# HGRN products of a head in eight small heaps behind half chunks instead of four behind whole chunks

## The chip, the cores and the metric

The kernel runs on one core of one Trainium2 chip. The metric is the device time of one execution in microseconds (us), median over runs; lower is better. TensorE (PE in the rows) does the matmuls, VectorE (DVE), ScalarE (ACT) and GpSimd (POOL) the elementwise work, and SyncE (SP) issues the large transfers.

## The reference, cut to what matters

The reference is one step of a two-layer decoder trunk over 512 prompt tokens and 8 sample tokens (520 columns, two halves of 260). The change touches one of its blocks, the HGRN2 mixer of the second layer: a projection to q, f, i and g, a gated linear recurrence with a 128x128 state for each of 8 heads, a norm and an output projection.

```python
def hgrn2_mixer(x, s0, lb, w_in, norm_g, w_out):
    proj = (x @ w_in).astype(f32)
    q, fz, i_in, g = jnp.split(proj, [HG_WIDTH, 2 * HG_WIDTH, 2 * HG_WIDTH + HG_HEADS * HG_DV], axis=-1)
    q = jax.nn.silu(q)
    logf = jnp.logaddexp(jnp.log(lbf), jnp.log1p(-lbf) + jax.nn.log_sigmoid(fz))
    k = -jnp.expm1(logf)
    o, s_fin = hgrn2_chunked(heads(q, HG_DK), heads(k, HG_DK), heads(i_in, HG_DV), heads(logf, HG_DK), s0)
    o = rmsnorm(o, norm_g).reshape(bsz, t, HG_HEADS * HG_DV) * jax.nn.silu(g)
    return o.astype(x.dtype) @ w_out, s_fin.astype(s0.dtype)
...
def step(s, inp):
    bcum = jnp.cumsum(gc, axis=1)
    o_inter = jnp.einsum('bthk,bhkv->bthv', qc * jnp.exp(bcum), s)
    att = jnp.einsum('bthk,bshk,btshk->bhts', qc, kc, decay)
    o_intra = jnp.einsum('bhts,bshv->bthv', att, vc)
    k_dec = kc * jnp.exp(btot[:, None] - bcum)
    s_new = jnp.exp(btot)[..., None] * s + jnp.einsum('bshk,bshv->bhkv', k_dec, vc)
```

`step` is the body of `hgrn2_chunked`, run over 8 chunks of 64 tokens with the state carried from one to the next.

## The kernel before

All activations lie feature by token. A projection is done in **chunks** of 128 output features; `chunk` (L2490 and on) does the two token halves of a chunk, 8 k-tiles with 3 matmuls of 260 columns each (high times high, low times high, high times low part), so 24 matmuls per half and 48 per chunk, into one of two pairs of PSUM banks (`lin`, j = 0 or 1). Before a chunk starts, its weights must be loaded (SP), copied to `w_hi` (ACT, `split`) and subtracted to `w_lo` (DVE, `split`, counted in `lo_ready`), and the last result in its banks must be taken out (`used[j]`).

In the HGRN block the engines each run a loop `hg_in` over h, written by hand as one straight program. Step h projects head h in four chunks, which give f, q, i and g in that order (DVE takes them out at L1896 to `t`, L1929 to `hgQ`, L1963 to `hgV` and L1998 to `hgG`). Beside this it does the products of head g = h-1 and the last ones of head e = h-2. These products are plain fp32 matmuls in **groups**, each filling one PSUM bank of `mis`:

- V, K: transposes of i and of the decayed k, copied out by ACT (L1487).
- S: the sample tokens' outputs, 8 matmuls with one column each.
- A0 to A3: q times k inside blocks of 32, 16 and 8 tokens and on the diagonal (L2378 three times, L2384), put under a mask into `attn` by DVE (L1918).
- D0, D1: k times v for 8 blocks of 64 tokens, from which DVE forms the running state `hS` in a chain of 8 steps (L1969, L1973).
- B0, B1: v of the sample tokens, spread, which DVE adds to the states `sS` (L1986).
- O: the output (L2393, L2399), copied out by ACT (L1530).
- N: sums of squares for the norm, one column each. R, r: the root spread over partitions, multiplied in by DVE (L1889).

**The order of groups** is the list `made` for `HG`, and PE must fill them in this order. There are four banks, used in turn: `Groups.reuse` makes PE wait before group q until group q-4 has been taken out by its owner (`void_dve` or `void_act`). PE's program puts the groups behind whole chunks: S and A0 to A3 behind the first, V, K, N behind the second, D and B behind the third, O, R, r behind the fourth. A run of groups between projection matmuls is called a **heap** here. DVE and ACT take the groups out at fixed places of their own straight programs. For h = 8 and 9 there is no projection left and the groups follow each other directly; the output projection (`hg_out`) comes after.

Of the kernel before, what the change touches and what calls it, by code (L numbers as in the profile page):

```python
# [12 lines left out]
P = 128  # L13
# [114 lines left out]
def trunk_kernel(nc, i_, o_):  # L128
# [408 lines left out]
    for h in range(HH + 2):  # L537
        g, e = h - 1, h - 2
        if 0 <= e < HH:
            made += [("S", e, "dve")]  # L540
        if 0 <= g < HH:
            made += [("A", (g, u), "dve") for u in range(len(LEVELS) + 1)] + [("V", g, "act"), ("K", g, "act")]
        if 0 <= e < HH:
            made += [("N", e, "act")]
        if 0 <= g < HH:
            made += [("D", (g, 0), "dve"), ("D", (g, 1), "dve"), ("B", (g, 0), "dve"), ("B", (g, 1), "dve")]
            made += [("O", g, "act")]
        if 0 <= e < HH:
            made += [("R", e, "dve"), ("r", e, "dve")]
    HG = Groups(made, hg["fill"], {"dve": hg["void_dve"], "act": hg["void_act"]}, banks=4)  # L550

# [85 lines left out]
    with block:  # L637
# [565 lines left out]
        def _(act):  # L1203
# [246 lines left out]
            def hg_in():  # L1450
# [3 lines left out]
                for h in range(HH + 3):  # L1454
                    g, e, d, p, b = h - 1, h - 2, h - 3, p0 + 2 * h, h % 2
                    if h < HH:
                        split(p, 1, KD)
                        if h == 0:
                            root(norm_of["hg_in", 1])
                            act.wait_ge(hg["lb"], 1)  # L1460
                        act.wait_ge(used[0], p + 1)
                        wait(act, gated, 2 * h)
                        if h >= 2:
                            act.wait_ge(hg["s_state"], 2 * (h - 1))
                            act.wait_ge(hg["scaled_pool"], POOLS * (h - 1))
                            act.wait_ge(hg["scaled_dve"], h - 1)
                        act.activation(hgF[:], t3[:], ACT.Sigmoid)
                        act.activation(hgK[b][:], t3[:], ACT.Sigmoid, scale=-1.0).then_inc(f_out, 1)
# [9 lines left out]
                    if h < HH:  # L1478
# [3 lines left out]
                        split(p + 1, 1, KD)  # L1482
                    if 0 <= g < HH:
                        for what, dst in (("V", vTok), ("K", kTok)):
                            q = G.at(what, g)
                            act.wait_ge(hg["fill"], q + 1)
                            act.activation(dst[:].rearrange("p a b -> p (a b)"), hg_bank(q), ACT.Copy)\  # L1487
                                .then_inc(hg["void_act"], 1)
                    if 0 <= e < HH:
# [85 lines left out]
        def _(dve):  # L1575
# [298 lines left out]
            def hg_in():  # L1874
# [3 lines left out]
                def halves(t, level):  # L1878
                    return t.rearrange("p q (b a t) -> p q b a t", a=2, t=level)[:, :, :, 1, :]

                for h in range(HH + 3):
                    g, e, d, p, b = h - 1, h - 2, h - 3, p0 + 2 * h, h % 2
# [18 lines left out]
                    if 0 <= g < HH:  # L1901
                        if g:
                            dve.wait_ge(hg["fill"], G.at("O", g - 1) + 1)
                        else:
                            dve.wait_ge(hg["consts"], 1)
                        for u, level in enumerate(LEVELS + (None,)):
                            q = G.at("A", (g, u))
                            dve.wait_ge(hg["fill"], q + 1)
                            if u:
                                dve.wait_ge(hg["void_dve"], G.before(q, "dve"))  # L1910
                            m = pair_mask[:, u:u + 1, :].bitcast(I32)
                            if level is None:
                                dst, src, m = attn[:], hg_bank(q).rearrange("p (q t) -> p q t", q=4), m.to_broadcast([P, 4, P])
                            else:
                                dst, m = halves(attn[:], level), halves(m, level)
                                m = m.to_broadcast([P, 4, P // (2 * level), level])
                                src = hg_bank(q)[:, 0:SEQ // 2].rearrange("p (q b t) -> p q b t", q=4, t=level)
                            dve.copy_predicated(dst, m, src).then_inc(hg["void_dve"], 1)  # L1918
                    if 0 <= e < HH:
# [3 lines left out]
                    if h < HH:  # L1923
# [9 lines left out]
                        dve.wait_ge(gate_out, g0 + 2 * h + 1)  # L1933
                        dve.tensor_tensor(hgQ[b][:], hgQ[b][:], t2[:], ALU.mult).then_inc(gated, 1)
                    if 0 <= e < HH:
                        G.emptied_of(dve, "N", e)
# [6 lines left out]
                    if h < HH:  # L1943
                        split(p + 1, 1, KD)
                        dve.wait_ge(hg["log"], h + 1)
                        if h:
# [133 lines left out]
        def _(pe):  # L2080
# [362 lines left out]
            def hg_in(chunk):  # L2443

                p0 = first_pair["hg_in", 1]
                for h in range(HH + 2):
                    g, e, p = h - 1, h - 2, p0 + 2 * h
                    if h < HH:
                        chunk(p, 0, h == 0)
                    if h == 0:  # L2450
                        pe.wait_ge(kv_ev2, KV * DEPTH)
                    if 0 <= e < HH:
                        hg_group("S", e)
                    if 0 <= g < HH:
                        for u in range(len(LEVELS) + 1):
                            hg_group("A", (g, u))
                    if h < HH:
                        chunk(p, 1, False)
                    if 0 <= g < HH:
                        hg_group("V", g)  # L2460
                        hg_group("K", g)
                    if 0 <= e < HH:
                        hg_group("N", e)
                    if h < HH:
                        chunk(p + 1, 0, False)
                    if 0 <= g < HH:
                        for what in ("D", "B"):
                            for f in range(2):
                                hg_group(what, (g, f))
                    if h < HH:  # L2470
                        chunk(p + 1, 1, False)
                    if 0 <= g < HH:
                        hg_group("O", g)
                    if 0 <= e < HH:
                        hg_group("R", e)
                        hg_group("r", e)
                HG.all_emptied(pe, len(HG.groups))

            def stream(n):
# [9 lines left out]

                def chunk(p, j, first):  # L2490
                    pe.wait_ge(lo_ready, 2 * p + j + 1)
                    wait(pe, used[j], p)
                    for half in range(2):
                        cols = slice(half * HT, (half + 1) * HT)
                        for k in range(kt):
                            if first and half == 0:
                                pe.wait_ge(x_done, x0 + k + 1)
                            for u, (w, x) in enumerate(((w_hi, x_hi), (w_hi, x_lo), (w_lo, x_hi))):
                                ins = pe.matmul(lin[:, j, half, 0:HT], w[:, j, k, :], x[:, k, cols],  # L2499
                                                start=k == 0 and u == 0, stop=k == kt - 1 and u == 2)  # L2500
                    ins.then_inc(chunk_done, 1)
                    if first and r == 0:
# [57 lines left out]
```

## Time and profile before

| | us |
|---|---|
| median of 3 runs | 2648.4 |
| lowest, highest run | 2644.25, 2656.82 |
| the profiled execution | 2662.53 |
| its span in the trace | 2660.8 |
| TensorE busy | 2537.1 |
| VectorE busy | 1267.4 |
| ScalarE busy | 829.8 |
| GpSimd busy | 610.9 |
| mean granted TensorE clock | 0.968 |

The profiled execution is one execution; its trace covers its span, which is 1.7 us shorter than its own time. The HGRN block's projections start at 1708.92 us of the span, and `hg_out` starts at 2042.84. The granted clock is the share of full TensorE speed that the chip grants: 1.00 is 2.4 GHz, 0.50 is 1.2 GHz.

### The profile page before, as it was taken

What the parts mean: (1) busy time and instruction counts of PE and PEld (TensorE: products, weight loads), DVE (VectorE), ACT (ScalarE), POOL (GpSimd) and SP (SyncE); (2) the same over time, 40 slices, a digit from 0 to 9 for tenths busy, and PEclk for the clock granted to TensorE, in tenths of its full rate; (3) what the DMA queues carried; (4) which work ended last, traced back from release to release, by engine and by line L of the source; (5) the groups of instructions that cost most, each with busy time, mean ns of one, the idle gap of its engine ahead of it and who ended that gap; (6) DMA issues with size and microseconds to landing.
All of it is one profiled execution on the core that took longest, in us unless ns stands there. A gap on an engine that the chain in (4) does not pass through costs nothing.

```text
span 2660.8 us, 48881 instructions
## 1 busy us (share of the span) xinstructions
PE 2537.1 (95%) x20589; PEld 2447.2 (92%) x20589; DVE 1267.4 (48%) x1783; ACT 829.8 (31%) x1196; POOL 610.9 (23%) x604
## 2 busy tenths in 40 slices
PE   6999999888989999999999999999999999999998
PEld 6999998777976999999999999999999968999997
DVE  4553543924445543344443344556655564442444
ACT  3322231433222322222332233355544232221221
POOL 5588747230201100002111011222211203000002
PEclk8999999899989999999999999998988999999998
DMA  7245444452364233233443333232231543332331
GB/s 156 80 158 127 121 120 130 133 169 76 92 216 126 85 90 103 81 97 114 125 120 104 97 95 111 82 89 82 66 89 50 163 169 97 91 101 84 88 101 65
DMA packets 479667, 289.10 MB, mean 109 GB/s; under 512 B 22352, under 2 KB 467024, under 8 KB 478480
## 3 DMA queue, kind: packets, MB, share of 16 engines
q1 hardware_dynamic: 473760, 280.66, 35.9%
q0 software_dynamic: 848, 1.89, 0.7%
q10 hardware_dynamic: 4896, 4.20, 0.5%
q8 instruction: 124, 2.03, 0.3%
q14 instruction: 39, 0.32, 0.0%
HBM read 258.86 MB, written 27.85 MB: 108 GB/s over the span
## 4 chain that ended last, share of the span: by engine, by line
PE 86%; DVE 7%; ACT 3%; DMA 2%; issue 2%; POOL 0%; SPq 0%; ACTq 0%; POOLq 0%; DVEq 0%
PE lin L2499 70%; PE mis L2124 3%; DVE w_lo L1583 1%; PE mis L2378 1%; ACT w_hi L1212 1%; DMA raw<-in_s_w_glu_dram 1%; DVE rstd L1596 1%; PE mis L2243 1%; PE mis L2228 1%; DVE a_lo L1589 1%; PE mis L2421 1%; DMA raw<-in_xattn_w_q_dram 1%; PE mis L2178 1%; PE lin L2243 1%; PE mis L2384 1%
## 5 line engine op out<-in xcount | busy, mean ns | idle before, releaser
L2499 PE MATMUL lin<-a_hi,w_hi 128*128 128x260 f32 x3584 | 1029.0, 287 | 39.1 <-DVE w_lo L1583 34.7
L2499 PE MATMUL lin<-a_lo,w_hi 128*128 128x260 f32 x3584 | 1019.5, 284 | 0.0
L2499 PE MATMUL lin<-a_hi,w_lo 128*128 128x260 f32 x3584 | 1018.8, 284 | 0.0
L2499 PEld LDWEIGHTS lin<-a_hi,w_hi 128*128 128x128 f32 x3584 | 682.8, 191 | 46.8 <-DVE w_lo L1583 31.9
L1583 DVE TENSOR_TENSOR w_lo<-raw,w_hi 128x1024 fp32r<-128x1024 f32 (+1 forms) x328 | 496.3, 1513 | 436.8 <-ACT w_hi L1212 434.7
L2499 PEld LDWEIGHTS lin<-a_lo,w_hi 128*128 128x128 f32 x3584 | 683.1, 191 | 0.2
L2499 PEld LDWEIGHTS lin<-a_hi,w_lo 128*128 128x128 f32 x3584 | 683.0, 191 | 0.0
L2499 PE MATMUL lin<-h_hi,w_hi 128*128 128x260 f32 x2048 | 580.8, 284 | 8.2 <-DVE h_lo L1805 3.3
L2499 PE MATMUL lin<-h_hi,w_lo 128*128 128x260 f32 x2048 | 580.1, 283 | 0.0
L2499 PE MATMUL lin<-h_lo,w_hi 128*128 128x260 f32 x2048 | 579.4, 283 | 0.0
L1212 ACT ACTIVATE w_hi<-raw 128x1024 fp32r<-128x1024 f32 (+1 forms) x328 | 364.3, 1111 | 343.5 <-PE lin L2499 304.9
L2499 PEld LDWEIGHTS lin<-h_hi,w_hi 128*128 128x128 f32 x2048 | 387.8, 189 | 10.8 <-issue 6.0
L2499 PEld LDWEIGHTS lin<-h_hi,w_lo 128*128 128x128 f32 x2048 | 387.7, 189 | 0.0
L2499 PEld LDWEIGHTS lin<-h_lo,w_hi 128*128 128x128 f32 x2048 | 387.4, 189 | 0.0
L968 POOL TENSOR_TENSOR acc<-xT 128x520 f32<-128x520 f32 x8 | 9.8, 1224 | 966.2 <-DVE xT L2047 923.3
L2047 DVE SCALAR_TENSOR_TENSOR xT<-lin,xT 128x520 f32<-128x520 f32 (+1 forms) x88 | 61.5, 699 | 302.2 <-PE lin L2499 302.2
L1547 ACT ACTIVATE h_hi<-t 128x520 fp32r<-128x520 f32 (+1 forms) x88 | 56.2, 639 | 433.5 <-DVE t L2031 433.5
L1544 ACT ACTIVATE t<-t 128x520 f32<-128x520 f32 x88 | 56.5, 642 | 308.0 <-DVE t L2025 308.0
L2029 DVE TENSOR_TENSOR t<-lin,rstd 128x520 f32<-128x520 f32 x88 | 61.5, 699 | 177.2 <-PE lin L2499 177.2
L970 POOL TENSOR_TENSOR sqt<-xT 128x520 f32 (+1 forms) x56 | 74.5, 1330 | 254.5 <-DVE xT L2047 186.2
L2025 DVE TENSOR_TENSOR t<-lin,rstd 128x520 f32<-128x520 f32 x88 | 61.5, 699 | 108.4 <-PE lin L2499 108.2
L1221 ACT ACTIVATE a_hi<-xT,vec 128x520 fp32r<-128x520 f32 (+1 forms) x56 | 40.2, 729 | 230.4 <-DVE xT L2047 198.7
(429 smaller groups left out, 2670.8 us busy)
## 6 DMA issues: line engine op xcount, KB each, us to landing
raw<-in_ffn_w_in_dram SPq DMA_DIRECT2D x176, 512.0 KB, 3.8
raw<-in_ffn_w_out_dram SPq DMA_DIRECT2D x64, 704.0 KB, 4.6
kc<-in_cache_mem_k_dram SPq DMA_DIRECT2D x32, 512.0 KB, 4.9
vc<-in_cache_mem_v_dram SPq DMA_DIRECT2D x16, 1024.0 KB, 7.3
raw<-in_hg_w_in_dram SPq DMA_DIRECT2D x32, 512.0 KB, 4.0
raw<-in_xattn_w_kv_dram SPq DMA_DIRECT2D x16, 512.0 KB, 4.1
raw<-in_s_w_glu_dram SPq DMA_DIRECT2D x16, 512.0 KB, 4.2
raw<-in_xattn_w_q_dram SPq DMA_DIRECT2D x16, 512.0 KB, 4.7
```

Source lines behind the costliest of these rows:

```text
L970: step.link(pool.tensor_tensor(sqt[:], tile(xT, m), tile(xT, m), ALU.mult))
L1212: act.activation(w_hi[:, j, 0:kt, :], raw[:, j, 0:kt, :], ACT.Copy).then_inc(hi_ready, 1)
L1221: act.activation(tile(a_hi, m), tile(xT, m), ACT.Copy, scale=vec[:, bass.ds(row + m, 1)]).then_inc(a_hi_done, 1)
L1544: act.activation(t2[:], t1[:], ACT.Silu).then_inc(gate_out, 1)
L1547: act.activation(tile(h_hi, i), t3[:], ACT.Copy).then_inc(h_hi_done, 1)
L1583: dve.tensor_tensor(w_lo[:, j, 0:kt, :], raw[:, j, 0:kt, :], w_hi[:, j, 0:kt, :].bitcast(F32), ALU.subtract).then_inc(lo_ready, 1)
L2025: dve.tensor_tensor(two(t1[:]), lslot(0), two(rstd[:]), ALU.mult).then_inc(used[0], 1)
L2029: step.link(dve.tensor_tensor(two(t4[:]), lslot(1), two(rstd[:]), ALU.mult))
L2047: dve.scalar_tensor_tensor(out=twotile(xT, m), in0=lslot(j), scalar=scale, in1=twotile(xT, m), op0=ALU.mult, op1=ALU.add)\
L2124: ins = pe.matmul(kv_bank(c)[:, 0:NM], w[:, e, k, :], x[:, k, :], start=k == 0 and u == 0, stop=k == KD - 1 and u == 2)
L2243: ins = pe.matmul(bank, vM[layer][:, m, (2 * h + e) * P:(2 * h + e + 1) * P], pT[:, h % 2, m, :], start=m == 0, stop=m == 1)
L2499: ins = pe.matmul(lin[:, j, half, 0:HT], w[:, j, k, :], x[:, k, cols], start=k == 0 and u == 0, stop=k == kt - 1 and u == 2)
```

## The change

PE's loop now places groups behind half chunks. `chunk` takes the halves to do, waits for weights and banks only with the first, and counts the chunk as done only with the second. The order of groups becomes V, K | S | A0, A1 | A2, N | A3, D0, D1 | B0, B1 | R, r | O, in eight heaps behind the eight halves of a step. Along with it ACT copies V and K out at the start of its step, ahead of the sigmoids of f, and DVE does the mask copies of A0 and A1 where all four stood, that of A2 after q is gated and that of A3 ahead of the clamp of log f. The number of matmuls, copies, banks and transfers is the same.

```diff
@@ made, the order of groups
     for h in range(HH + 2):
         g, e = h - 1, h - 2
+        if 0 <= g < HH:
+            made += [("V", g, "act"), ("K", g, "act")]
         if 0 <= e < HH:
             made += [("S", e, "dve")]
         if 0 <= g < HH:
-            made += [("A", (g, u), "dve") for u in range(len(LEVELS) + 1)] + [("V", g, "act"), ("K", g, "act")]
+            made += [("A", (g, u), "dve") for u in range(len(LEVELS))]
         if 0 <= e < HH:
             made += [("N", e, "act")]
         if 0 <= g < HH:
+            made += [("A", (g, len(LEVELS)), "dve")]
             made += [("D", (g, 0), "dve"), ("D", (g, 1), "dve"), ("B", (g, 0), "dve"), ("B", (g, 1), "dve")]
-            made += [("O", g, "act")]
         if 0 <= e < HH:
             made += [("R", e, "dve"), ("r", e, "dve")]
+        if 0 <= g < HH:
+            made += [("O", g, "act")]
...
@@ ACT, hg_in
                     if h < HH:
                         split(p, 1, KD)
+                    if 0 <= g < HH:
+                        for what, dst in (("V", vTok), ("K", kTok)):
+                            q = G.at(what, g)
+                            act.wait_ge(hg["fill"], q + 1)
...
@@ DVE, hg_in (causal(g, u) is the old body of the loop over u)
-                        for u, level in enumerate(LEVELS + (None,)):
...
+                        for u in range(2):
+                            causal(g, u)
...
                         dve.tensor_tensor(hgQ[b][:], hgQ[b][:], t2[:], ALU.mult).then_inc(gated, 1)
+                    if 0 <= g < HH:
+                        causal(g, 2)
...
                     if h < HH:
                         split(p + 1, 1, KD)
+                    if 0 <= g < HH:
+                        causal(g, 3)
+                    if h < HH:
                         dve.wait_ge(hg["log"], h + 1)
...
@@ PE, hg_in (mine: 0 <= g < HH, older: 0 <= e < HH)
+                    def projected(i, half):
+                        if h < HH:
+                            chunk(p + i // 2, i % 2, h == 0 and i == 0, (half,))
...
+                    projected(0, 0)
+                    if mine:
+                        hg_group("V", g)
+                        hg_group("K", g)
+                    projected(0, 1)
+                    if older:
+                        hg_group("S", e)
+                    projected(1, 0)
+                    if mine:
+                        hg_group("A", (g, 0))
+                        hg_group("A", (g, 1))
+                    projected(1, 1)
+                    if mine:
+                        hg_group("A", (g, 2))
+                    if older:
                         hg_group("N", e)
+                    projected(2, 0)
+                    if mine:
+                        hg_group("A", (g, 3))
+                        hg_group("D", (g, 0))
+                        hg_group("D", (g, 1))
+                    projected(2, 1)
+                    if mine:
+                        hg_group("B", (g, 0))
+                        hg_group("B", (g, 1))
+                    projected(3, 0)
+                    if older:
                         hg_group("R", e)
                         hg_group("r", e)
+                    projected(3, 1)
+                    if mine:
+                        hg_group("O", g)
...
@@ chunk
+                def chunk(p, j, first, halves=(0, 1)):
+                    if 0 in halves:
+                        pe.wait_ge(lo_ready, 2 * p + j + 1)
+                        wait(pe, used[j], p)
+                    for half in halves:
...
+                    if 1 not in halves:
+                        return
                     ins.then_inc(chunk_done, 1)
```

Two places of the compiled order follow. On PE, in the step of a middle head, before the change the S group (matmuls on `hgQ` and `sS`) and all four A groups stand in one heap between projection matmuls on `a_hi`, `a_lo`:

```order
L2499 MATMUL lin<-a_hi,w_lo 128x260
L2426 MATMUL mis<-hgQ_140,sS_157 128x1 x8
L2378 MATMUL mis<-lvl_160 128x64 x4
L2378 MATMUL mis<-lvl_161 128x64 x4
L2378 MATMUL mis<-lvl_162 128x64 x4
L2384 MATMUL mis<-dgQ,dgK 128x128 x4
L2499 MATMUL lin<-a_hi,w_hi 128x260
```

With the change, in the same place, 24 projection matmuls (one half, left out as "...") lie between S, A0 with A1, and A2 with N:

```order
L2440 MATMUL mis<-hgQ_141,sS_158 128x1 x8
...
L2392 MATMUL mis<-lvl_160 128x64 x4
L2392 MATMUL mis<-lvl_161 128x64 x4
...
L2392 MATMUL mis<-lvl_162 128x64 x4
L2446 MATMUL mis<-ones,hgS 128x1 x4
L2446 MATMUL mis<-ones,hgS 8x1
...
L2398 MATMUL mis<-dgQ,dgK 128x128 x4
```

The heap of S and A0 to A3 has become four heaps with projection between them, the last of them shared with D0 and D1.

On ACT, before the change the copies of V and K (`vTok`, `kTok`) stand between the sigmoid of q with the split behind it and the root, scaling and logarithm that end in `bC`:

```order
L1481 ACTIVATE t_64<-hgQ_140 128x520
L1212 ACTIVATE w_hi<-raw 128x1024
L1487 ACTIVATE vTok<-mis 128x512
L1487 ACTIVATE kTok<-mis 128x512
L1494 ACT_TABLE_LOAD
L1494 ACTIVATE rT<-mis,eps 128x4
L1495 ACTIVATE rT<-mis,eps 8x1
L1499 ACTIVATE hgK_142<-hgK_142,lbv 128x520
L1501 ACT_TABLE_LOAD
L1501 ACTIVATE bC<-hgF,lbv 128x512
```

With the change they stand at the start of the step, behind the copy of the last head's output (`hO`) and the split for the second chunk:

```order
L1535 ACTIVATE hO<-mis 128x512
L1216 ACTIVATE w_hi<-raw 128x1024
L1466 ACTIVATE vTok<-mis 128x512
L1466 ACTIVATE kTok<-mis 128x512
L1478 ACTIVATE hgF<-t_65 128x520
L1479 ACTIVATE hgK_142<-t_65 128x520
```

The stretch from the sigmoid of q to `bC` has become shorter by two copies. The copy of `hO`, which waits for group O, still stands ahead of the split for the second chunk, while group O itself has moved to the end of PE's step.

## Rows read from the trace of the kernel before

**Rows 1.** The page: granted clock in tenths of full speed, 40 equal slices of the span.
```profile
PEclk8999999899989999999999999998988999999998
```

**Rows 2.** Busy by stretch (start:end length, busy, counts, PEclk, DMA): whole head steps.
```profile
1730.00:1765.00 35.00, 35.00 (x300) 34.74 (x299) 24.00 (x41) 22.80 (x38) 15.91 (x15) 1.00 0.28 79
1765.48:1806.55 41.07, 41.07 (x324) 40.62 (x324) 23.78 (x50) 21.46 (x36) 8.49 (x9) 0.92 0.28 79
...
1929.58:1970.57 40.99, 40.99 (x324) 40.55 (x323) 24.56 (x51) 21.90 (x37) 7.68 (x9) 0.92 0.29 80
```

**Rows 3.** The same view: stretches of low clock, first and last shown, six in all.
```profile
1774.00:1780.80 6.80, 6.80 (x34) 6.80 (x33) 2.68 (x5) 0.99 (x2) 0.00 (x0) 0.50 0.46 128
...
1978.90:1985.60 6.70, 6.70 (x33) 6.70 (x33) 2.20 (x5) 1.59 (x3) 0.00 (x0) 0.50 0.35 97
```

**Rows 4.** The same view: D, B; O, R, r; the steps without projections.
```profile
1834.50:1838.00 3.50, 3.50 (x34) 3.37 (x33) 3.14 (x7) 3.48 (x11) 0.00 (x0) 1.00 0.53 150
1843.80:1847.50 3.70, 3.70 (x34) 3.58 (x32) 3.15 (x10) 0.60 (x1) 3.70 (x3) 1.00 0.06 18
...
2007.00:2047.00 40.00, 36.50 (x226) 35.37 (x225) 20.88 (x52) 12.74 (x26) 4.82 (x4) 0.70 0.15 44
```

**Rows 5.** Chain that ended last (start, length, what), step of h = 1.
```profile
1737.95 2.62 PE mis L2378 x24
1740.58 0.95 PE mis L2384 x8
1741.52 5.73 PE lin L2499 x48
```

**Rows 6.** The same view, step of h = 3.
```profile
1812.55 1.68 PE mis L2426 x16
1814.22 4.45 PE mis L2378 x24
1818.68 1.81 PE mis L2384 x8
1820.49 6.39 PE lin L2499 x48
1826.88 0.87 PE mis L2408 x8
1827.75 0.91 PE mis L2432 x10
1828.66 5.92 PE lin L2499 x48
```

**Rows 7.** Instructions in order of time (start, length, engine, line), DVE, step of h = 4.
```profile
1867.91 0.70 DVE L1929 TENSOR_TENSOR hgQ<-lin,rstd 128x520 f32<-128x520 f32 x1 [3.71 <-PE lin L2499]
...
1875.67 0.43 DVE L1948 TENSOR_SCALAR bC<-bC 128x512 f32<-128x512 f32 x1 [0.79 <-ACT bC L1501]
...
1884.54 1.22 DVE L1583 TENSOR_TENSOR w_lo<-raw,w_hi 128x1024 fp32r<-128x1024 f32 x1 [0.24 <-DVE hS L1973]
```

**Rows 8.** The same view, ACT, from the same step.
```profile
1850.14 0.58 ACT L1530 ACTIVATE hO<-mis 128x512 f32<-128x512 f32 x1
1850.62 1.05 ACT L1212 ACTIVATE w_hi<-raw 128x1024 fp32r<-128x1024 f32 x1
...
1870.13 0.57 ACT L1487 ACTIVATE vTok<-mis 128x512 f32<-128x512 f32 x1
...
1871.21 1.28 ACT L1494 ACT_TABLE_LOAD   x1
```

**Rows 9.** The same view, PE: the first matmuls of a chunk behind a heap, full clock.
```profile
1741.28 0.37 PE L2499 MATMUL lin<-a_hi,w_hi 128*128 128x260 f32 x1
1741.48 0.28 PE L2499 MATMUL lin<-a_lo,w_hi 128*128 128x260 f32 x1
1741.60 0.28 PE L2499 MATMUL lin<-a_hi,w_lo 128*128 128x260 f32 x1
```

**Rows 10.** The same view, POOL, from the step of h = 4: outK scaled.
```profile
1886.31 1.26 POOL L1179 TENSOR_TENSOR outK<-outK,hgK 128x512 f32<-128x512 f32 x1
```

More of the change, by code:

```diff
@@ L1457, in hg_in @@
                         split(p, 1, KD)
+                    if 0 <= g < HH:
+                        for what, dst in (("V", vTok), ("K", kTok)):
+                            q = G.at(what, g)
+                            act.wait_ge(hg["fill"], q + 1)
+                            act.activation(dst[:].rearrange("p a b -> p (a b)"), hg_bank(q), ACT.Copy)\
+                                .then_inc(hg["void_act"], 1)
+                    if h < HH:
                         if h == 0:
@@ L1482, in hg_in @@
                         split(p + 1, 1, KD)
[L1483 to L1488, printed above, removed]
                     if 0 <= e < HH:
@@ L1879, in halves, with causal @@
                     return t.rearrange("p q (b a t) -> p q b a t", a=2, t=level)[:, :, :, 1, :]
+                def causal(g, u):
+                    q = G.at("A", (g, u))
+                    dve.wait_ge(hg["fill"], q + 1)
+                    if u:
+                        dve.wait_ge(hg["void_dve"], G.before(q, "dve"))
+                    m = pair_mask[:, u:u + 1, :].bitcast(I32)
+                    if u == len(LEVELS):
+                        dst, src, m = attn[:], hg_bank(q).rearrange("p (q t) -> p q t", q=4), m.to_broadcast([P, 4, P])
+                    else:
+                        level = LEVELS[u]
+                        dst, m = halves(attn[:], level), halves(m, level)
+                        m = m.to_broadcast([P, 4, P // (2 * level), level])
+                        src = hg_bank(q)[:, 0:SEQ // 2].rearrange("p (q b t) -> p q b t", q=4, t=level)
+                    dve.copy_predicated(dst, m, src).then_inc(hg["void_dve"], 1)
                 for h in range(HH + 3):
@@ L1905, in hg_in @@
                             dve.wait_ge(hg["consts"], 1)
-                        for u, level in enumerate(LEVELS + (None,)):
[L1907 to L1918, printed above, removed]
+                        for u in range(2):
+                            causal(g, u)
                     if 0 <= e < HH:
@@ L2447, in hg_in @@
                     g, e, p = h - 1, h - 2, p0 + 2 * h
[L2448 to L2458, printed above, removed]
@@ L2459, in hg_in @@
-                    if 0 <= g < HH:
+                    mine, older = 0 <= g < HH, 0 <= e < HH
+                    def projected(i, half):
+                        if h < HH:
+                            chunk(p + i // 2, i % 2, h == 0 and i == 0, (half,))
+                            if h == 0 and i == 0 and half == 1:
+                                pe.wait_ge(kv_ev2, KV * DEPTH)
+                    projected(0, 0)
+                    if mine:
                         hg_group("V", g)
                         hg_group("K", g)
-                    if 0 <= e < HH:
-                        hg_group("N", e)
@@ L2464, in hg_in @@
[L2464 to L2474, printed above, removed]
+                    projected(0, 1)
@@ L2488, in stream @@
                     x_done, x0 = a_lo_done, KD * split_norms.index(r_in)
[L2490 to L2493, printed above, removed]
+                def chunk(p, j, first, halves=(0, 1)):
[3 more added lines that the diff above has]
+                    for half in halves:
                         cols = slice(half * HT, (half + 1) * HT)
```

## The prediction

> **What bounds the kernel now.** I read the clock over the span first: it is below full speed in the slices of the HGRN block too, though these are full of work [rows 1]. Then the busy time by head step. The reader should see two things there. TensorE is busy for all of a step (41.07 of 41.07 us, 40.99 of 40.99), so no other engine holds it up; and its mean granted clock is 0.92, against 1.00 in the step of h = 1, which has no S heap yet [rows 2]. Cut finer, each step of h = 2 to 7 has one stretch of about 6.8 us at 0.50, that is at 1.2 GHz instead of 2.4, six in all, about 41 us apart [rows 3]. It begins inside the heap of S and A0 to A3. What TensorE did before it fell: 1.68 us of matmuls with one column each and then matmuls of 64 columns, behind a chunk at full clock [rows 6]. It fell behind no other heap of a step: D with B kept 1.00 for 3.5 us, O with R and r for 3.7 us [rows 4], and in the step of h = 1 A0 to A3 without S kept it too [rows 2]. So it takes thin and very thin products together to make it fall, and it is TensorE's own time, at a clock that it loses once a head, that bounds this block.
>
> The price of one fall is read by setting the same work at either clock side by side: the three levels of A 4.45 us against 2.62, the diagonal 1.81 against 0.95, the chunk behind it 6.39 against 5.73 [rows 5, 6]. That is 1.83 + 0.86 + 0.66 = 3.35 us. A step without it would be 41.0 - 3.3 = 37.7 us.
>
> **Part 1, the clock.** The change puts a half chunk, 2.9 us of dense matmuls (half of 5.8), between S (1.7 us) and A0 with A1 (two thirds of 2.62, 1.75 us), and again ahead of A2 with N (0.87 + 1.0 us). The thinnest heap is now S alone or N with A2, under 1.9 us, with dense work on both sides. V, K and N in one heap of 1.8 us, N's 0.91 us of single columns in it [rows 6], did not bring the clock down in these steps, and A without S, 2.62 + 0.95 us in the step of h = 1, did not either [rows 2, 5]. S alone is nearly twice N's length, and no row shows it alone between chunks; the nearest row is V, K, N, and I take no fall. Saved: six falls at 3.3 us, 19.8 us. The bounds are 0 (each head still falls once) and 19.8. The two steps without projections (h = 8, 9; mean clock 0.70 [rows 4]) keep their thin groups back to back, so their falls stay.
>
> The Trainium skill, "TensorE: Matmul & The Clock Gate", section "HAM oscillation — how this bites in real kernels", puts the fall of the clock down to idle gaps of TensorE. The trace differs: TensorE shows no idle time in steps whose clock falls [rows 2, 3]. By that rule alone nothing is there for the change to mend, and the first term would be 0; this is rival 2 below.
>
> **Part 2, more seams.** The first matmul of a chunk behind a heap takes 0.20 us to the next one's start, the second 0.12 [rows 9], so a seam costs 0.08 us, the way back into the heap I put at nothing or the same again. Four more seams in a step are 0.3 to 0.6 us; I take 0.4, and in the seven steps with heaps and chunks 2.8 us.
>
> **Part 3, a new wait for R.** With four banks R takes the bank of D0, which comes free only when DVE has finished the whole chain of `hS`. From the take-out of q to the clamp of log f are 7.76 us (1867.91 to 1875.67), from there to the end of the chain 8.87 (1884.54) [rows 7]. ACT's copies of V and K, 1.08 us (1870.13 to 1871.21), leave the first stretch [rows 8]; the mask copy of A3, 0.7 us, comes into DVE's part of it but fits in the 0.79 us for which DVE waited there [rows 7], and A3 itself is filled just in time: behind the second chunk come A2, N, half a chunk and A3 (0.9 + 1.0 + 3.0 + 0.9 = 5.8 us), while the logarithm comes 6.7 us behind q. So the bank is free 15.55 us after q, 15.75 after the second chunk's end (0.2 us from the end of a chunk to DVE's start). TensorE wants it after A2, N, half, A3 with D, half, B, half: 0.87 + 0.95 + 2.95 + 2.5 + 2.95 + 1.85 + 2.95 = 15.0, with seams 15.1. It waits 0.6 us. Bounds: 0, if 0.6 us of the chain goes; 1.5 if the split for g's weights and A3's copy come late.
>
> **Part 4, a new wait for K.** K takes the bank of R, which DVE empties behind the split for the second chunk, which needs ACT's `w_hi`, which stands behind ACT's copy of O. O now ends PE's step. From there: 0.25 us to ACT, the copy of O 0.5 and `w_hi` 1.0 (starts 1850.14, 1850.62, length 1.05 [rows 8]), the split 1.15, the product with R 0.7, together 3.65 to 3.7. PE has half a chunk and V, 2.95 + 0.45 = 3.4. It waits 0.3 us. Behind K in PE's queue stands the second half of the f chunk, so DVE's take-out of f and the sigmoids behind it move by the same 0.3 us. K's other input, outK scaled by POOL, came 19.7 us behind the take-out of q (1887.57 less 1867.91) [rows 7, 10]; K is now wanted 15.1 us (to R) + 1.3 + 2.95 + 2.4 + 2.95 + 0.45 = 25.2 us behind it, so 5 us of TensorE's own work hide that it is wanted earlier; with that cover gone each us would cost one per head.
>
> The two waits come from one loop, from the second chunk's end over `hS` to the next second chunk, so they are paid in each of the six steps: 0.9 x 6 = 5.4 us. Bounds 0 and 1.8 x 6 = 10.8.
>
> **Part 5, the rest.** DMAs are the same, SP's sample states wait for S, which now ends 0.9 us later in the step, with a step's time of cover. POOL's work is unchanged and waits for ACT only. The steps without projections hold the same chain V, K, A, D, B, O, then S, N, R in 35 us, in a new order; I put them at 0, with 2 us either way.
>
> **Sum for the profiled execution.** 2662.5 - 19.8 + 2.8 + 5.4 = 2650.9 us, a step of 37.7 + 0.4 + 0.9 = 39.0 us.
>
> **From there to a median.** The profiled execution is 14.1 us above the median and above all three runs, which themselves spread by 12.6 us. One fall is 3.3 us, so the spread is about four falls. One trace does not show how near to the edge they are; I read the spread as heads with and without a fall: the profiled execution had six of six, the median run fewer. Time that the timed runs lack for this reason cannot be saved again. If all 14.1 us are falls (4 of 6), the changed kernel's median is 2650.9; if none is, and it is what the profiling adds, it is 2636.8. The spread speaks for falls, and I take two thirds: 2650.9 - 4.9 = 2646.0. So the forecast is no difference that can be told, because what is saved in the falls is partly absent from the timed runs and partly paid back in seams and waits. A measurement of this kernel can tell about 0.5%, 13.2 us, from no change.
>
> **Rivals.**
> 1. The falls go and the waits do not come (the chain from q to `hS` 1 us shorter than I put it). A step is 38.1 us; 5.4 us less: 2640.6, and down to 2631.4 if the 14.1 us are profiling. For it: 0.6 and 0.3 us are small differences of sums of 15 and 4 us. Against: all their terms are rows.
> 2. **Slower:** the clock still falls once a head, at S or at one of the new seams, while seams and waits are paid. Its place is S with the half chunks around it; the price is the 2.8 + 5.4 = 8.2 us of parts 2 to 4, with nothing saved for it; against the profiled execution it decides once fewer than three of the six falls go (three are 9.9 us). Own time 2662.5 + 8.2 = 2670.7, median by the same two thirds 2665.8 at most, 2657 if the falls only stay as they are. For it: S's single columns last 1.7 us; also, the skill's page named above, section "A second HAM failure mode: psum-queue depth-cycling", says that waits between groups that cycle through PSUM banks make the clock go up and down, and the change adds two such waits. Against: V, K, N with single columns, and the trace's seams, without a fall [rows 4, 6]. I put it at 2664.
> 3. The falls go, and the loop of the two waits is 1.8 us a head, at the upper bound: 5.4 us more, 2651.4.
> 4. The saving is whole against the median, with waits as forecast: the profiled execution's 14.1 us are profiling, the timed runs had all their falls: 2637. For it: the clock stretches repeat so evenly. Against: three runs 12.6 us apart.
>
> That the change does not do what it says is excluded by the compiled order: S and the A groups are apart on TensorE.
>
> **How the numbers follow.** Forecast 0.42 (2640 to 2653), rival 1 0.13, rival 2 0.12, rival 3 0.11, rival 4 0.22. Faster by over 0.5% means under 2635.2: two fifths of rival 4, two fifths of rival 1 and 0.10 of the forecast, since the runs of before in the comparison may themselves lie high: together 0.24. Slower means over 2661.6, most of rival 2: 0.10. The rest, 0.66, is within 0.5%. The range runs from 2633, inside rivals 1 and 4, to 2659, the lower part of rival 2.
>
> **What the changed profile would show.** Right: no stretch at 0.50 between the start of the projections and the end of the seventh head's step, head steps of 38.5 to 39.5 us, TensorE idle ahead of R for about 0.6 us (released by DVE's `hS`) and ahead of K for 0.3 (by DVE's product with R), S followed by a chunk half at full clock. Wrong: a stretch at 0.50 that begins in or behind S (rival 2), steps of 38.1 (rival 1) or 40 (rival 3), or timed runs of the changed kernel that spread as widely as those of before, which would take the falls out of the reading of the spread.

## The result, and the profile after

| | before | changed |
|---|---|---|
| median of 18 runs | 2646.33 | 2658.86 |
| lowest, highest | 2640.60, 2656.82 | 2655.01, 2665.06 |
| profiled execution, span | 2660.8 | 2656.9 |
| its mean granted clock | 0.968 | 0.975 |

The changed kernel takes 1.0045 times the time of before (95% interval 1.0034 to 1.0057), 12.5 us by the medians. That is slower, and too little for the 0.5% that the prediction took as its bound. The profiled executions stand the other way round, 3.9 us in favour of the change. Both are true, and why is the point of this case. The forecast was 2646.0 us, 2.4 us under the median of before as it was then known; the changed kernel is 12.9 us above the forecast.

First the head steps of the changed kernel, in the view of busy time by stretch (start:end, length, busy time and count of PE, PE's weight loads, DVE, ACT, POOL, then clock, DMA share, GB/s). They answer to [rows 2] and [rows 4].

```profile
1802.30:1842.25 39.95, 38.31 (x324) 37.44 (x324) 25.81 (x52) 22.25 (x37) 8.10 (x8) 1.00 0.29 82
1842.25:1882.19 39.94, 38.34 (x325) 37.46 (x324) 25.79 (x52) 22.25 (x37) 8.10 (x8) 1.00 0.29 81
...
2002.09:2036.50 34.41, 29.76 (x168) 28.24 (x168) 13.90 (x39) 9.56 (x23) 0.00 (x0) 0.65 0.12 33
```

The clock is 1.00 in the steps: the falls of [rows 3] are gone. But TensorE is no longer busy throughout: 1.6 us of each of these two steps are idle by this count, and a step is 39.94 us, where before it was 41.0 with a fall. The third row is the steps without projections. Who is waited for stands in the view of waits, PE alone, 1800 to 1990 us (us in total, times, longest):

```profile
PE mis L2422 <- DVE hO L1909: 5.5, 5, 1.1
PE mis L2451 <- DVEq L1990: 2.0, 4, 0.5
```

L2422 are the transposes, here K; L1909 is DVE's product with R. L2451 is R; L1990 is the release of D0 and D1 behind the chain of `hS`. These are the two waits that the prediction named. The view counts less than what is lost, since a matmul's end is modelled; by start times the half chunk ahead of R takes 3.65 us instead of 2.97 (0.68 lost) and V with K 2.11 instead of 0.79 (1.3 lost). R waits in all six steps of h = 2 to 7, K in the five of h = 3 to 7: the step of h = 2 is 38.6 us, and V with K take 0.79 us in it.

Where K's wait comes from is read in the order of time of three engines ahead of it, in the same step. DVE:

```profile
1839.56 1.05 DVE L2009 TENSOR_TENSOR dgQ<-dgQ,hgQ 128x512 f32<-128x512 f32 x1 [0.24 <-DVE sS L2000]
1840.53 1.75 DVE L2010 TENSOR_TENSOR dgK<-dgK,hgK 128x512 f32<-128x512 f32 x1
1842.21 0.69 DVE L2012 TENSOR_TENSOR hgG<-lin,rstd 128x520 f32<-128x520 f32 x1
...
1845.04 1.22 DVE L1588 TENSOR_TENSOR w_lo<-raw,w_hi 128x1024 fp32r<-128x1024 f32 x1 [0.73 <-ACT w_hi L1216]
1846.18 0.75 DVE L1909 TENSOR_TENSOR hO<-hO,mis 128x512 f32<-128x512 f32 x2
```

ACT:

```profile
1842.93 0.64 ACT L1531 ACTIVATE t<-hgG 128x520 f32<-128x520 f32 x1 [5.01 <-DVE hgG L2012]
1843.47 0.58 ACT L1535 ACTIVATE hO<-mis 128x512 f32<-128x512 f32 x1
1843.95 1.05 ACT L1216 ACTIVATE w_hi<-raw 128x1024 fp32r<-128x1024 f32 x1
```

POOL and PE:

```profile
1840.03 1.71 POOL L1185 TENSOR_TENSOR inQ<-inQ,hgQ 128x512 f32<-128x512 f32 x1
...
1845.22 0.60 PE L2422 MATMUL mis<-ident,hgV 128*128 128x128 f32 x4
1846.91 0.66 PE L2422 MATMUL mis<-ident,outK 128*128 128x128 f32 x4 [1.09 <-DVE hO L1909]
```

PE's step ended with O at 1842.25. ACT's copy of O (L1535) began only 1.22 us later, since the sigmoid of g stands ahead of it and waits for DVE's take-out of g (L2012), which stands behind dgK; and dgK took 1.75 us, beside POOL's inQ with 1.71. In the kernel before, inQ was over before dgK began, and each was quicker:

```profile
1887.54 1.26 POOL L1181 TENSOR_TENSOR inQ<-inQ,hgQ 128x512 f32<-128x512 f32 x1
1889.27 0.68 DVE L1996 TENSOR_TENSOR dgK<-dgK,hgK 128x512 f32<-128x512 f32 x1
```

From the copy of O the way is as the prediction has it: split on ACT, split on DVE, product with R, K.

### The profile page after: what moved, and what is told of

It reads as the page before. It is cut to its first block, busy times and chain, and to the rows that moved or that the text cites. A ratio compares the mean times of both kernels' runs of the same rounds, so it can differ in the third digit from the quotient of the medians.

```text
span 2656.9 us, 48880 instructions
## 1 busy us (share of the span) xinstructions
PE 2520.5 (95%) x20589; PEld 2427.4 (91%) x20589; DVE 1275.5 (48%) x1783; ACT 831.8 (31%) x1196; POOL 614.8 (23%) x604
## 4 chain that ended last, share of the span: by engine, by line
PE 80%; DVE 10%; ACT 4%; DMA 3%; issue 2%; POOL 1%; SPq 0%; ACTq 0%; DVEq 0%; POOLq 0%
PE lin L2525 66%; PE mis L2138 3%; ACT w_hi L1216 1%; DVE w_lo L1588 1%; PE mis L2392 1%; DMA raw<-in_s_w_glu_dram 1%; PE mis L2257 1%; DMA raw<-in_ffn_w_in_dram 1%; DVE a_lo L1594 1%; DVE hS L1987 1%; DVE rstd L1601 1%; PE mis L2242 1%; DMA raw<-in_xattn_w_q_dram 1%; PE mis L2440 1%; PE mis L2192 1%
```

## The experiments

The medians of a group belong to the executions of before on the same chip: e0, e1, e3, e6 beside 2651.8 (35 runs), e4, e7, e8, e9 beside 2645.2 (27 runs), e10 beside 2648.4 (17 runs).

| kernel | us | ratio to before (95%) | step in its profile |
|---|---|---|---|
| e0, before again | 2649.87 | 1.0002 (0.9970 to 1.0034) | 37.8, one of 39.4 |
| e4, changed again | 2658.24 | 1.0042 (1.0024 to 1.0060) | 39.9 |
| e1, product with R first | 2653.07 | 0.9995 (0.9965 to 1.0025) | 38.6 |
| e6, R, r behind O | 2648.33 | 0.9974 (0.9946 to 1.0002) | 37.8 |
| e7, inQ on 8 columns | 2651.33 | 1.0018 (0.9998 to 1.0037) | 39.0 |
| e3, S between halves | 2644.70 | 0.9962 (0.9931 to 0.9994) | 37.8 |
| e10, the same | 2643.74 | 0.9977 (0.9959 to 0.9995) | 37.8 |
| e8, S twice in the heap | 2679.07 | 1.0123 (1.0088 to 1.0158) | 44.4 |
| e9, S twice between halves | 2666.56 | 1.0080 (1.0057 to 1.0103) | 39.6 to 42.7 |

### e0: the kernel before, again

No edit.

> The kernel before, unchanged, for the granted clock and span of each execution. Theory F (falls differ from execution to execution): the mean clock is not the same in all executions; with six falls of 6.8 us at half clock the profiled execution had 0.968, each fall less adds 6.8 x 0.5 / 2660.8 = 0.0013, so a median run at 2646 should show about 0.973 (two falls) and the slowest ones 0.969. Theory P (what is missing is profiling overhead): all timed executions show 0.968 to 0.969 and six falls, and the profile of this kernel is again some 14 us above its own timed median.

Its profiled execution has a span of 2641.9 us, 18.9 less than the one shown ahead of the prediction, from the same program. Busy time by stretch: two middle steps, the sixth (h = 7), the steps without projections, and the stretch of the only fall in the six:

```profile
1764.34:1802.14 37.80, 37.80 (x325) 37.36 (x324) 24.22 (x52) 21.38 (x36) 8.41 (x9) 1.00 0.31 86
1802.14:1839.93 37.79, 37.79 (x323) 37.35 (x323) 24.60 (x51) 21.90 (x37) 7.71 (x9) 1.00 0.31 87
1953.24:1992.65 39.41, 39.41 (x323) 38.97 (x322) 24.57 (x51) 21.90 (x37) 7.71 (x9) 0.96 0.29 83
1992.65:2023.83 31.18, 27.66 (x168) 26.70 (x167) 15.18 (x40) 9.81 (x23) 0.24 (x1) 0.69 0.18 54
1963.40:1966.80 3.40, 3.40 (x18) 3.40 (x17) 1.61 (x3) 0.00 (x0) 0.00 (x0) 0.50 0.32 97
```

Five steps of 37.8 us without a fall, and one short fall in the sixth, against six of six in the first trace. So the falls are a matter of the execution. The clocks of all executions agree: among the 35 of before on this chip, the six quickest (2640.1 to 2643.9) had 0.975 to 0.978, the five slowest (2670.8 to 2676.0) 0.962 to 0.965. Theory F stands and theory P falls. Why one execution has the falls and another has not is open. Falls are not all of the spread either: the time outside the HGRN block goes from 2319.7 (e8) to 2330.1 us (e1) in the eleven profiles of this document, though nothing there was changed. The slowest executions lie some 13 us above what six falls of 3.3 us explain from 2643; no trace caught one of them, so what made them so long is open too.

### e4: the changed kernel, again

No edit.

> The changed kernel, unchanged, for the clock of each of its executions beside those of before and beside the other kernels on the same chip. Theory (no falls in its steps, two waits in each): steps of 39.9 us in the profile, times within 10 us of each other, and 12 to 15 us above those executions of before that had no fall (2643 us, clock 0.975 to 0.976). Rival (its steps lose clock in some executions too): clocks down to 0.965 among its executions, as before has them.

Steps 39.93 to 39.97 us, no stretch at 0.50 in them; executions from 2655.1 to 2663.9 with clocks 0.972 to 0.977, where those of before on the same chip went from 2638.5 (0.977) to 2665.1 (0.967). Median less median 13.0 us. The theory holds: the changed kernel lost the clock in none of these steps in either profile, and pays more than the falls cost most executions of before.

### e1: the product with R ahead of the split

```diff
@@ DVE, hg_in
-                    if h < HH:
-                        split(p, 1, KD)
                     if 0 <= d < HH:
                         for what, cols in (("R", slice(0, SEQ)), ("r", slice(SEQ, NT))):
...
+                    if h < HH:
+                        split(p, 1, KD)
```

> The changed kernel with one edit: DVE multiplies R and r in ahead of the split for the second chunk, not behind it, so K's bank no longer waits for ACT's copy of O and the two splits. Theory K (the loop over R's bank makes the 1.2 us in front of K): that wait goes, the steps fall from 39.9 to 38.7 us and 6 x 1.2 = 7 us are saved, to about 2651.5. Rival (K waits for something else, the V transposes or POOL's outK): the wait stays and the time does not move.

Steps and PE's waits of this kernel:

```profile
1813.83:1852.45 38.62, 38.11 (x324) 37.48 (x323) 25.81 (x50) 22.14 (x37) 8.10 (x8) 1.00 0.30 85
```

```profile
PE mis L2451 <- DVEq L1990: 2.6, 5, 0.5
```

The wait ahead of K is gone, the one ahead of R stays, and a step is 38.6: 1.3 us less, as theory K has it. dgK still takes 1.75 us here, and costs nothing of K's any more. The median is 5.8 us below that of the 18 runs of the changed kernel above, taken apart from these, where 7 were expected.

### e6: R and r behind O

```diff
@@ made
-        if 0 <= e < HH:
-            made += [("R", e, "dve"), ("r", e, "dve")]
         if 0 <= g < HH:
             made += [("O", g, "act")]
+        if 0 <= e < HH:
+            made += [("R", e, "dve"), ("r", e, "dve")]
@@ PE, hg_in
                     projected(3, 0)
-                    if older:
-                        hg_group("R", e)
-                        hg_group("r", e)
                     projected(3, 1)
                     if mine:
                         hg_group("O", g)
+                    if older:
+                        hg_group("R", e)
+                        hg_group("r", e)
```

> The changed kernel with R and r behind O again, as before, in list and program; the seven other heaps stay as changed. R then follows D0 by six groups instead of four, and K follows O by four, V follows B1 by five. Theory (both new waits come from the order of banks): neither wait is left, steps of 38.1 us, 6 x 1.85 = 11 us less than the changed kernel, 2648, and no falls. Rival: what was waited for at R comes back as a wait of O for the state (chain of hS), 0.6 us a head, so 7 us less, 2652.

```profile
1809.39:1847.19 37.80, 37.80 (x324) 37.37 (x323) 25.80 (x50) 22.16 (x37) 8.09 (x8) 1.00 0.31 86
1847.19:1885.01 37.82, 37.82 (x324) 37.39 (x323) 25.78 (x50) 22.15 (x37) 8.09 (x8) 1.00 0.31 86
```

TensorE is busy throughout, and a step is 37.8 us (38.1 were expected), as the steps of e0 that have no fall, with seven heaps instead of four. dgK takes 1.75 us here too, off the path. So both waits came from the order of banks alone, no wait for the state took their place, and the three additional seams cost next to nothing (37.81 against 37.78). The whole block (from the first projection to `hg_out`) still takes 319.9 us against 316.1 in e0, which has a fall of 1.6 us in it; this is outside the steps, below.

### e7: POOL's inQ on 8 columns

This kernel leaves 504 of the 512 columns of inQ unscaled, so it computes something else and serves for its times alone.

```diff
-                    pool.tensor_tensor(inQ[e][:], inQ[e][:], hgQ[e][:, 0:SEQ], ALU.mult).then_inc(hg["scaled_pool"], 1)
+                    pool.tensor_tensor(inQ[e][:, 0:8], inQ[e][:, 0:8], hgQ[e][:, 0:8], ALU.mult).then_inc(hg["scaled_pool"], 1)
```

> The changed kernel with POOL's product of inQ done on 8 of 512 columns, so the rest of inQ stays unscaled and 1.5 us of POOL's work leaves each step. Theory C (DVE's product of dgK takes 1.75 us instead of 0.68 because POOL's inQ runs beside it, and this delays the take-out of g, the sigmoid, ACT's copy of O, the splits, the product with R and so K): dgK back at 0.7 to 0.9 us, the wait ahead of K 1.3 us becomes 0.3, steps of 38.9 us, 6 us less in the whole kernel. Rival (dgK's length is not on the way to K, ACT's copy of O waits for O alone): the wait ahead of K stays at 1.3 and the steps at 39.9.

The view by tile, DVE's product of dgK (min, median, max ns), here and then in the changed kernel, and one step of this kernel:

```profile
L2010 DVE TENSOR_TENSOR dgK<-dgK,hgK x8: 682/684/1223, 1731.9 to 1998.8; 128x512 f32<-128x512 f32 x8
```

```profile
L2010 DVE TENSOR_TENSOR dgK<-dgK,hgK x8: 1225/1754/1774, 1728.6 to 2000.4; 128x512 f32<-128x512 f32 x8
```

```profile
1812.65:1851.64 38.99, 38.35 (x324) 37.48 (x324) 24.73 (x50) 22.34 (x37) 7.04 (x8) 1.00 0.29 84
```

dgK is back at 0.68 us, and a step is 1.0 us shorter. ACT's copy of O and PE's V and K, same step:

```profile
1844.89 0.60 ACT L1535 ACTIVATE hO<-mis 128x512 f32<-128x512 f32 x1
```

```profile
1847.63 0.60 PE L2422 MATMUL mis<-ident,hgV 128*128 128x128 f32 x4
1848.34 0.66 PE L2422 MATMUL mis<-ident,outK 128*128 128x128 f32 x4
```

O ended at 1844.66, so its copy starts 0.23 us behind it instead of 1.22. K starts 0.71 us behind V, where 0.44 is the time without a wait: about 0.3 us of K's wait are left, though the view of waits no longer shows them. So 1 us of K's 1.3 us is this collision of DVE and POOL, and the rest is what the prediction had. The median is 6.9 us below e4's on the same chip. In the profiles the five steps in which K waits are 4.9 us shorter together, and the steps without projections take 30.9 us instead of 34.4.

### e3 and e10: the kernel before with S between the halves

```diff
@@ PE, hg_in of the kernel before; chunk with halves as in the change
                     if h < HH:
-                        chunk(p, 0, h == 0)
-                    if h == 0:
-                        pe.wait_ge(kv_ev2, KV * DEPTH)
+                        chunk(p, 0, h == 0, (0,))
                     if 0 <= e < HH:
                         hg_group("S", e)
+                    if h < HH:
+                        chunk(p, 0, h == 0, (1,))
+                    if h == 0:
+                        pe.wait_ge(kv_ev2, KV * DEPTH)
```

> The kernel before with one edit: S stands between the two halves of the first chunk instead of at the head of the heap of S and A. No other group moves and the order of banks stays. Both theories: no stretch at 0.50 in the steps of h = 2 to 7, no idle time of TensorE, a head step of 37.8 us. Theory F: against the kernel before it saves only the falls that its timed runs have, two of six, 7 us, and its runs spread less. Theory P: it saves 19 us against the timed runs of before. If the clock falls nevertheless (S with 1.7 us of single columns is enough), the time stays as before and the reading of the falls is wrong.

> The kernel before with S between the halves of the first chunk, once more, beside new executions of before. Its gain is what the falls of before are worth, and this differs with how many of them an execution has. If falls are a matter of the execution, this kernel has no clock under 0.972 among its executions while before has some, its fastest executions are only 1 to 3 us below the fastest of before, and its median is 2 to 6 us below the median of before. If it has no real gain, the medians agree within 1 us.

```profile
1804.50:1842.32 37.82, 37.82 (x324) 37.38 (x323) 24.54 (x51) 21.92 (x38) 7.69 (x8) 1.00 0.32 87
1917.93:1955.72 37.79, 37.79 (x325) 37.35 (x324) 24.50 (x51) 21.86 (x38) 7.70 (x8) 1.00 0.31 86
```

```profile
1801.87:1839.66 37.79, 37.79 (x324) 37.34 (x323) 24.52 (x51) 21.91 (x38) 7.69 (x8) 1.00 0.31 87
```

The first two are steps of e3, the third is one of e10. No falls in any step of either, no idle time, steps of 37.8. Both times it is faster than before, 0.9962 and 0.9977, with intervals under 1: 7.1 and 4.7 us by the medians. Its executions go from 2639.7 to 2649.9 and from 2640.5 to 2650.7, where those of before reached 2676.0 and 2663.1 beside it. Its quickest ones are within 1.5 us of the quickest of before. No execution of either has a clock under 0.972. This is theory F again: what it saves is the falls, and only where they come. The gain is small, 0.2 to 0.4%, but it was measured twice, and this version beats both kernels.

### e8 and e9: a longer thin stretch

```diff
-                    for b in range(NS):
+                    for b in 2 * list(range(NS)):
                         ins = pe.matmul(bank[:, b:b + 1], sS[a % 2][:, b, :], hgQ[a % 2][:, SEQ + b:SEQ + b + 1],
                                         start=True, stop=True)
```

In e8 in the kernel before, in e9 in e3.

> The kernel before with each matmul of S issued twice (same results), so 1.7 us more of single columns ahead of A0 to A3 in every step with S. Theory F (whether the clock falls depends on how the thin stretch comes to lie; a longer one falls always): a fall in each of the six steps in every execution, steps of 37.8 + 1.7 + 3.4 = 42.9 us at least, the times 8 x 1.7 + 6 x 3.3 = 33 us above the executions of before without a fall, about 2676, and closer together than those of before. If falls stay a matter of the execution, the profile has fewer than six and the times spread over 20 us.

> The kernel before with S between the halves of the first chunk, each of its matmuls issued twice: 3.4 us of single columns, with 2.9 us of dense work ahead and behind. If what stands around S protects the clock, no falls and steps of 37.8 + 1.7 = 39.5 us, 14 us above the same placement with S once. If the length of the thin stretch decides, it falls in some or all steps, 2 to 3.4 us each, whatever stands behind the halves. I expect falls in most steps: two thin stretches of 1.7 us do not fall, one of 3.4 does.

First e8, the stretches of the first two falls, then three steps of e9 in a row:

```profile
1768.20:1778.20 10.00, 10.00 (x48) 10.00 (x48) 2.07 (x5) 1.74 (x3) 0.00 (x0) 0.50 0.35 101
1812.60:1822.60 10.00, 10.00 (x48) 10.00 (x48) 2.04 (x5) 1.81 (x3) 0.00 (x0) 0.50 0.24 70
```

```profile
1767.00:1806.60 39.60, 39.60 (x341) 39.16 (x340) 23.81 (x49) 22.25 (x38) 7.69 (x8) 1.00 0.34 91
1806.60:1847.70 41.10, 41.10 (x340) 40.66 (x339) 24.50 (x51) 21.87 (x38) 7.69 (x8) 0.96 0.28 79
1847.70:1890.40 42.70, 42.70 (x340) 42.26 (x339) 24.48 (x51) 21.86 (x38) 7.69 (x8) 0.92 0.27 76
```

In e8 all six steps have a fall, five of them at 0.50 for 10 us instead of 6.8, and a step is 44.4: 37.8 + 1.7 + 4.9. I had expected 42.9 at least, so the size of a fall is not fixed. Its times, 2677.0 to 2690.1, lie wholly above all of before beside it. In e9 one of six steps had no fall, the others falls of 3.4 or 6.8 us. So the length of the thin stretch matters: with dense halves on both sides 3.4 us of single columns brought the clock down in five of six steps, 1.7 us in no step of any profile here (e3, e10, e1, e4, e6, e7, the changed kernel). That the halves alone protect the clock is wrong.

## Why the prediction was wrong, point by point

**What bounds the kernel.** Right for the profiled execution: TensorE at a clock that falls. Wrong as a picture of the kernel: e0, the same program, has 37.8 us steps. The first trace happened to hold six falls of six.

**Part 1, the clock.** The mechanism was right, no fall in any step of the changed kernel, its repetition, e1, e6 and e7. The price of 3.3 us was right too (41.0 against 37.8). That it takes very thin and thin products together was too narrow: in e9 single columns alone, twice as many, made it fall between dense halves.

**From there to a median.** Here is the first step that failed. The prediction counted two thirds of the 14.1 us between profile and median as falls that the timed runs lacked (a third of 14.1 is 4.7 and not 4.9, which moves the forecast by 0.2 us). That left 10.6 us to gain on a median: 19.8 less 9.2. e3 and e10 measured what there was to gain, 7.1 and 4.7 us, and for the executions of the first table it was about 4.5 (below). By estimate the median execution of before has one or two falls in these steps and not the three of the forecast; no trace of a median execution shows them. e0 shows that falls can make up all of such a gap: 17.8 of the 18.9 us between its span and the first one's lie in the HGRN block. Rival 4 with its 0.22 was the wrong end altogether. The argument from the spread was weak as well: the prediction read 12.6 us between three runs as about four falls, but the changed kernel's runs span 10.1 us and e3's 10.3, without a fall in these steps in their profiles.

**Part 2, seams.** 0.4 us a step taken, 0.03 measured for three of the four (e6 against e0); in the changed kernel 0.16 us of a step are left for all four (39.94 less 37.78, 0.68 and 1.32). Two start times gave a price per seam that did not carry over; V with K take 0.79 us instead of 0.87 in a heap of their own, so part of it comes back there.

**Part 3, the wait for R.** 0.6 taken, 0.68 measured; e6 removed it by the bank order. Right.

**Part 4, the wait for K.** 0.3 in each of six steps taken, 1.3 in each of five measured. This is the second step that failed, and the larger one. The mechanism, R's bank behind copy of O, splits and product, was right (e1 removed it). The term that failed is its first one, "0.25 us to ACT": it measured 1.22. The copy of O does not start when O is filled but behind the sigmoid of g, and so behind DVE's dgK, and that product grew from 0.68 to 1.75 us beside POOL's inQ. The other terms hold: the numbers as written add up to 3.6 us from O's end to K, and e7, where the copy starts after 0.23 us, has 3.68 (1844.66 to 1848.34). As the rows read, ACT's split for the next step's first chunk now waits 1.43 us for the third chunk; ACT's exponentials and POOL's products behind it come 1.6 us later against DVE's chain than before (POOL's first product 1.6 us ahead of the chain's end, before 3.2), and so reach into dgK. That this wait is the cause was read, not tried. The prediction wrote that POOL's work is unchanged and looked only at when it is ready, not at what runs beside it. e7 measured the collision by itself: 1.0 us a step. The trace of before had the like of it, in the same head step, beside the split of [rows 7] at 1884.54: POOL's product took 1.74 us there, its neighbours 0.74, and DVE's split was no longer than elsewhere.

The split's wait on ACT in the changed kernel, then POOL's long product in the kernel before:

```profile
1870.32 1.06 ACT L1216 ACTIVATE w_hi<-raw 128x1024 fp32r<-128x1024 f32 x1 [1.43 <-PE lin L2525]
```

```profile
1884.60 1.74 POOL L1177 TENSOR_TENSOR lvl<-lvl,hgK 128x256 f32<-128x256 f32 x1
```

**Part 5, the rest.** 0 taken with 2 us either way; it is 5.3 us, the third step that failed. The step of h = 1 takes 2.1 us longer (58.75 us from the block's start to that step's end, against 56.6), since K of head 0 is wanted early and POOL's outK is late; the steps without projections take 34.4 us against 31.2 (in e0). About 1.1 us of these 3.2 are waits: K's wait for R's bank takes 2.1 us there, and all of PE's waits together 4.6 against 3.5. The other 2.1 us are the clock, 0.65 on average against 0.69: behind K's wait the S group runs at the lower level. It takes 3.30 us there, where it took 1.95 in e0. PE's waits, 1725 to 1760 us and then 2000 to 2037 us of the changed kernel:

```profile
PE mis L2422 <- POOL outK L1183: 2.0, 1, 2.0
```

```profile
PE mis L2422 <- DVE hO L1909: 2.1, 1, 2.1
```

S in the first step without projections, the changed kernel and then e0:

```profile
2005.27 3.30 PE L2440 MATMUL mis<-hgQ,sS 128*128 128x1 f32 x16
```

```profile
1992.65 1.95 PE L2426 MATMUL mis<-hgQ,sS 128*128 128x1 f32 x16
```

**The balance.** Between the two first profiles: steps of h = 2 to 7 246.1 us against 238.4, so -7.7; step of h = 1 +2.1; the end +3.2; together -2.4 (333.9 to 331.5 us), where the prediction had -11.6. Against e0, an execution of before with one short fall: 331.5 less 316.1, +15.4 us, in a span that is 15.0 us longer. The medians are 12.5 us apart. Without e0's fall of 1.6 us the change costs 17.0 us in the block, so some 4.5 us of falls are left to a median execution of before; this is an estimate, since it sets spans beside medians.

The forecast was 2.4 us faster, the result 12.5 slower. Of these 14.9 us 8.8 are costs (17.0 instead of 8.2: 3.9 in the six steps, most of it K's wait with 6.5 instead of 1.8, and 4.9 outside them) and 6.1 the gain (4.5 instead of 10.6). Each of the two alone would have turned the forecast gain into a loss.

**The rivals.** None describes the result. Rival 3 had the waits at their upper bound and is the nearest, 1.8 us a step against 2.0 measured, but stood on the same reading of the median. Rival 2, the only one on the slower side, needed falls, and there were none: slower came with the clock mended.

## What to carry to other kernels

A clock that falls in one profiled execution may stay up in the next of the same program; before a saving is priced on it, the times and clocks of several executions have to show how often it is there. Where groups share a rotation of banks, moving one earlier also moves its wait to another owner, so each group's predecessor in its bank has to be followed through the programs of the engines that empty it, what stands ahead of that on each engine included, and with it what runs beside that on the engine next to it. The smallest edit that parts the thin work, one group moved by half a chunk, kept the clock and left all orders as they were; eight heaps bought nothing beyond it.

## What the runs showed of the hardware

- The granted clock fell to 0.50 with TensorE busy all of the time, and whether it did differed between executions of one program with the same work at the same places: six falls of 6.8 us, or one of 3.4.
- With single columns for 1.7 us and A behind them the clock fell in six of six steps of one profile and in one of six of another; with single columns for 3.4 us and A behind, in all six of e8's. Between dense halves it fell in none of twelve steps (e3, e10) with 1.7 us, and in five of six with 3.4 us (e9). The falls lasted 3.4, 6.8 or 10.2 us.
- DVE's product of two SBUF tiles took 1.75 us instead of 0.68 beside POOL's product (1.71 instead of 1.26 us), with the same operands; with POOL's part cut to 8 columns it was 0.68 again. Beside DVE's split in the kernel before, POOL's product took 1.74 us instead of 0.74, and the split its usual 1.22. The Trainium skill, "SBUF — State Buffer", section "Who interferes with whom", says that a DVE instruction with two SBUF inputs contends with a GpSimd instruction that reads SBUF. The traces agree: these products were longer where the other engine worked beside them. The price fell on both engines in the first pair and on POOL alone in the second.
